# A hybrid decoder layer in three passes over the tokens (128 and the samples, 128, 256) instead of two

## The chip, the cores and the metric

The kernel runs on one core of a Trainium2 chip. The metric is device time in microseconds, the median of several executions. Besides them one execution was profiled; every row shown here is from that one.

The engines are TensorE (PE in the rows, PEld its weight loads, PEq its sequencer), VectorE (DVE), ScalarE (ACT), GpSimd (POOL) and SyncE (SP, which here only starts DMAs).

## What is computed

One layer over 512 prompt tokens and 8 sample tokens, everything in float32, D = 2048. Shortened from the reference:

```python
proj = x @ w_in                                   # z, xbc, dt, u|v, gates
xbc = silu(causal_conv(xbc, conv_state))          # 4 taps
y_a, state = ssd_scan(x, dt, A, B, C, state)      # chunks of 128 tokens, 8 groups of 8 heads
y_a = rms_norm((y_a + d_skip * x) * silu(z))      # by group
u, v = split(gelu(uv));  v = layer_norm(v)
y_b = u * (tril(W_s) @ v + b)                     # within 128-token chunks
merged = g_a * (y_a @ w_branch_a) + g_b * (y_b @ w_branch_b)
h = layer_norm(ALPHA * x + merged @ w_out)
q = h @ w_q                                       # 8 heads, two halves of 128 keys
expert, gate = top16 of the 16 x 16 sums of both halves' top16
act = gelu(einsum('td,thkd->thk', h, peer_u[expert]))     # 128 experts a token
y = layer_norm(ALPHA * h + einsum('thk,thkd->td', gate * act, peer_v[expert]))
```

Of the prompt the final scan state, the last three convolution rows and the last chunk's v are returned too; of every sample the new convolution rows, the new scan state (64 heads x 64 x 128) and v.

## The kernel before

All products with weights are made with the features on the partitions: a weight tile is 128 output features by 2048 inputs, 1 MiB in HBM, and `gemm` (L399) makes 16 matmuls of it against the pass's tokens, which stand side by side in the free dimension. In the profile each such float32 matmul is two records, so a tile is 32. There are 224 tiles, and **each pass over the tokens reads all of them**: pass A has 256 prompt tokens and the 8 samples (264 columns), pass B the other 256.

A pass has three stages with a barrier behind each:

- `ssd` (80 tiles): for each of 8 groups six tiles of B, C and x, four of z; convolution on VectorE, and for each block of 128 tokens `chunk_a` and `chunk_b` on TensorE with `spread_chunk`, `weigh`, `next_state` and `outputs` on VectorE, and `decay` on ScalarE. Then the gating (L1137), its square (ScalarE, L1000), the mean square `rms` (L865) and `finish`. The names conv, weigh and so on stand in the code below.
- `sgu` (32 tiles): v, its layer norm, the spatial product, u.
- `back` (112 tiles): 32 gate tiles, 16 of branch B (`wb`), 32 of branch A (`wa`), 16 of the output (`out`), the layer norm, and 16 query tiles with scores and top-16 selection on VectorE. I call those last 16 tiles the query stage.

**Samples.** In pass A's scan GpSimd updates the samples' states in 64 units of 128 x 512 (eight a group): decay (L1193), B times x (L1195, from the tile BC_bcast), sum (L1197), store to HBM (L1198), product with C (L1201), which VectorE sums in `sum_smp`. The states' loads are issued by GpSimd too (`load`, L1164), two units ahead. BC_bcast is B and C of the samples, turned by TensorE (`turn_bc`, L833), copied by ScalarE (`keep_bc`), written to HBM by GpSimd (L1183) and read back to all partitions (L1185).

**Experts.** Each (block, j) item is a slot: GpSimd gathers 128 rows of peer_u and later 128 rows of peer_v (L250, 1 MiB each), VectorE makes the dot products (L306) and adds the weighted rows (L327). 260 of the 520 slots lie in pass B between its other work, at places that `plan` (L424) writes out; they belong to the tokens of pass A. GpSimd keeps four u rows and four v rows ahead. The other 260 come in the tail with eight rows each.

**Queues.** SyncE issues the weight tiles in the order of the passes (`load_weight`, L390): tile p + 3 after tile p's last matmul, into a ring of three. Between them, in the same order of issue, stand the loads of the decay rows, the stores of y and of the scan state, the branch activations for `wa` (`load_ya`), x (L534) and the keys. An instruction on SyncE that waits holds up all that follow.

## Time and profile before

| | |
|---|---|
| median of 3 runs | 5419.52 us (5419.21 to 5420.57) |
| the profiled execution | 5416.87 us |
| its span | 5414.9 us |
| TensorE busy, mean granted clock | 3608.6 us, 0.828 |
| VectorE busy | 3422.2 us |
| ScalarE busy | 702.4 us |
| GpSimd busy | 2398.3 us |
| DMA | 1672 MB, mean 309 GB/s |
| tables and constants | 0 to 56 us |
| pass A: scan, to the query stage, query stage | 56 to 780, to 1756, to 1938 |
| pass B: scan, spatial stage, gates to output, query stage | 1938 to 2762, to 3085, to 3862, to 4068 |
| tail: 260 expert slots | 4068 to 5415 |

No engine is busy over 67% of the span, because the stages have different limits. The table by stage is the one to read: for each stretch the busy time of each engine, TensorE's granted clock (1 is 2.4 GHz, 0.5 is 1.2 GHz), the share of the 16 DMA engines' time and what they moved.

### The profile page before, as it was taken

To read this page: it belongs to the slowest core of one execution; us is meant where nothing else is said; L and a number is where in the kernel's file an instruction comes from. 1 tells how busy PE (TensorE), PEld (TensorE's weight loads), DVE (VectorE), ACT (ScalarE), POOL (GpSimd) and SP (SyncE) were. 2 spreads that over 40 slices of the span, in tenths; PEclk is the share of its full clock that TensorE was granted. 3 is DMA by queue.
4 is the path that set the end of the run, shared out by engine and by line. 5 is a ranking of instruction groups with operands and counts; after the bars stand their busy time and mean duration, and the time that the engine had idled before them with its cause. 6 is when DMAs were issued, how large, how long until landed. Compare 5 with 4: busy or idle time off the path is not lost. (4 is left out here: it accounts for less than half of the span.)

```text
span 5414.9 us, 43573 instructions
## 1 busy us (share of the span) xinstructions
PE 3608.6 (67%) x16560; PEld 3028.1 (56%) x16560; DVE 3422.2 (63%) x4133; ACT 702.4 (13%) x1501; POOL 2398.3 (44%) x1504
## 2 busy tenths in 40 slices
PE   7999979999999968888778697897940000230000
PEld 5787768888887757667667586786740000000000
DVE  3455531000001859989867665565798999789999
ACT  2232321000000123333311010000100000000000
POOL 3575730000000025545543432443318888778885
PEclk8999989999999989999889898998975555565555
DMA  5565643344444379999989899999749999999998
GB/s 175 192 217 196 210 156 132 133 148 164 164 156 140 126 301 405 421 420 410 421 356 377 351 421 384 389 421 412 307 155 398 420 422 422 422 380 422 422 422 363
DMA packets 275097, 1672.07 MB, mean 309 GB/s; under 512 B 37041, under 2 KB 66225, under 8 KB 81969
## 3 DMA queue, kind: packets, MB, share of 16 engines
q0 software_dynamic: 161920, 1133.78, 51.2%
q1 hardware_dynamic: 112968, 535.51, 26.4%
q8 instruction: 131, 2.15, 0.2%
q14 instruction: 78, 0.63, 0.0%
HBM read 1633.31 MB, written 35.79 MB: 308 GB/s over the span
## 5 line engine op out<-in xcount | busy, mean ns | idle before, releaser
L250 POOL DMA_INDIRECT rows_a<-in_peer_u,expert x384 | 819.0, 2133 | 2182.4 <-POOLq L369 1149.2
L409 PE MATMUL psum<-rows_a,w_ring 128*128 128x264 f32 x7168 | 1625.5, 388 | 24.1 <-PEq L369 18.9
L409 PEld LDWEIGHTS psum<-rows_a,w_ring 128*128 128x128 f32 x7168 | 1367.2, 191 | 265.5 <-issue 30.5
L409 PE MATMUL psum<-x_acts,w_ring 128*128 128x256 f32 x5632 | 1257.4, 384 | 131.0 <-PEq L369 57.5
L409 PEld LDWEIGHTS psum<-x_acts,w_ring 128*128 128x128 f32 x5632 | 1084.0, 193 | 287.9 <-issue 83.4
L306 DVE SCALAR_TENSOR_TENSOR rows_a<-rows_a,h_tokens 128x2048 f32<-128x2048 f32 x384 | 878.7, 2289 | 106.1 <-DMA rows_a<-in_peer_u,expert 75.9
L250 POOL DMA_INDIRECT rows_a<-in_peer_v,expert x384 | 593.3, 1545 | 333.2 <-DVE h_tokens L327 165.1
L327 DVE SCALAR_TENSOR_TENSOR h_tokens<-rows_a,coef,h_tokens 128x2048 f32<-128x2048 f32 x256 | 602.6, 2354 | 79.4 <-issue 73.5
L1744 PE MATMUL psum<-acc,selector 8*128 8x512 f32 x64 | 57.5, 1075 | 683.8 <-DVE rows_a L306 479.0
L1744 PEld LDWEIGHTS psum<-acc,selector 8*128 8x128 f32 x64 | 19.9, 325 | 720.0 <-DVE rows_a L306 485.3
L1019 DVE SCALAR_TENSOR_TENSOR conv_acc<-raw,g_par,conv_acc 128x256 f32<-128x256 f32 x288 | 175.5, 609 | 283.8 <-ACT conv_acc L913 277.0
L327 DVE SCALAR_TENSOR_TENSOR acc<-rows_a,coef,acc 128x2048 f32<-128x2048 f32 x128 | 300.9, 2350 | 32.8 <-issue 30.2
L327 DVE SCALAR_TENSOR_TENSOR h_tokens<-rows_b,coef,h_tokens 128x2048 f32<-128x2048 f32 x128 | 300.9, 2351 | 20.2 <-issue 16.2
L306 DVE SCALAR_TENSOR_TENSOR rows_b<-rows_b,h_tokens 128x2048 f32<-128x2048 f32 x128 | 293.0, 2290 | 27.3 <-DMA rows_b<-in_peer_u,expert 22.6
L286 ACT ACTIVATE gelu<-dots 128x4 f32<-128x4 f32 x130 | 26.7, 205 | 2140.3 <-DVE rows_a L306 1517.1
L250 POOL DMA_INDIRECT rows_b<-in_peer_u,expert x128 | 265.5, 2074 | 81.5 <-issue 37.2
L250 POOL DMA_INDIRECT rows_b<-in_peer_v,expert x128 | 252.9, 1976 | 51.1 <-issue 37.4
L409 PE MATMUL psum<-branch_b,w_ring 128*128 128x256 f32 x1024 | 229.7, 385 | 43.6 <-DMA w_ring<-in_w_tiles 29.1
L409 PEld LDWEIGHTS psum<-branch_b,w_ring 128*128 128x128 f32 x1024 | 197.8, 194 | 72.6 <-issue 43.1
L1622 DVE TENSOR_TENSOR rows_a<-rows_a,psum 128x264 f32<-128x264 f32 x16 | 6.9, 429 | 338.3 <-PE psum L409 338.3
L1631 DVE TENSOR_TENSOR branch_part<-spare,psum 128x264 f32<-128x264 f32 x16 | 6.9, 429 | 214.2 <-PE psum L409 214.2
L409 PE MATMUL psum<-merged,w_ring 128*128 128x256 f32 x512 | 115.2, 384 | 1.8 <-DVE merged L1634 1.8
(368 smaller groups left out, 3024.8 us busy)
## 6 DMA issues: line engine op xcount, KB each, us to landing
w_ring<-in_w_tiles SPq DMA_DIRECT2D x448, 1024.0 KB, 6.3
smp_state<-in_state_ssm POOLq DMA_DIRECT2D x64, 256.0 KB, 5.7
out_ssm_sample<-smp_state POOLq DMA_DIRECT2D x64, 256.0 KB, 3.1
rows_a<-acum_rows_dram SPq DMA_DIRECT2D x16, 512.0 KB, 7.4
BC_bcast<-smp_bc_dram POOLq DMA_DIRECT2D x8, 1024.0 KB, 5.0
branch_b<-acum_rows_dram SPq DMA_DIRECT2D x16, 512.0 KB, 12.4
rows_a<-in_peer_u,expert POOLq DMA_INDIRECT x384, 20.6
rows_a<-in_peer_v,expert POOLq DMA_INDIRECT x384, 21.1
```

The costliest lines, as they stand in the source:

```text
L250: return pool.indirect_dma_start(out=dst, out_offset=None, in_=table, in_offset=bass.IndirectOffsetOnAxis(ap=self.index(s), axis=0))
L286: act.activation(self.ge[:, c], self.dots[:, c], ACT.Gelu).then_inc(self.gelu_done, 1)
L306: dve.scalar_tensor_tensor(out=u, in0=u, scalar=1.0, in1=h, op0=ALU.mult, op1=ALU.mult, accum_out=self.dots[:, s % 8:s % 8 + 1]).then_inc( ...
L327: dve.scalar_tensor_tensor(out=acc, in0=self.vrow[self.slot[s]], scalar=self.coef[:, s % 8:s % 8 + 1], in1=acc, op0=ALU.mult, op1=ALU.add) ...
L409: last = pe.matmul(o, self.w_ring[:, p % RING, k * P:(k + 1) * P], x[:, k, :], start=start and k == 0, stop=stop and k == KB - 1)
L1019: ins = dve.scalar_tensor_tensor(out=ac, in0=r[:, k:k + NP], scalar=w[:, k:k + 1], in1=ac, op0=ALU.mult, op1=ALU.add)
L1622: self.out_of_bank(dve.tensor_tensor(merged[:, m, :], merged[:, m, :], self.bank[(G_WB + m) % 2][:, 0:n], ALU.mult), G_WB + m)
L1631: self.out_of_bank(dve.tensor_tensor(part[:, m % 2, :], ga[:, m, :], self.bank[(G_WA + m) % 2][:, 0:n], ALU.mult), G_WA + m)
L1744: last = pe.matmul(self.bank[c], sel[:, b, :], h_smp[:, 512 * c:512 * (c + 1)], start=True, stop=True)
```

## The change

Everything computed stays the same. The passes are now 128 tokens with the samples (136 columns), 128 tokens, and 256 tokens. I call them A', B' and C'. The weight tiles are read three times. In passes A' and B' the ring has four slots (`w_more` is the fourth), in C' three. The 260 slots within passes are split: 80 in B', 180 in C' (`STEPS_B`, `STEPS_C`: scan per group, v, u, gates, wb, wa, output, layer norm, queries); the tail keeps its 260.

In a pass with one block, `chunk_b` stands behind the last z tile, and VectorE makes the next group's first convolution behind the gating instead of between the sums. The sample states' loads move from GpSimd to SyncE, between the weight tiles, up to four units ahead; the updates stay on GpSimd. The samples' selection is now made in pass B'.

```diff
-RING = 3
-PASSES = 2
+PASS_CHUNKS = ((0, 1), (1, 1), (2, 2))
+PASSES = len(PASS_CHUNKS)
+RINGS = (4, 4, 3)
+RING = max(RINGS)
...
+STEPS_B = (4, 4, 7, 8, 4, 8, 7, 2, 8)
+STEPS_C = (10, 12, 14, 22, 12, 22, 10, 2, 6)
...
-        if p >= PASSES * N_TILES:
-            return
-        if p >= RING:
-            sp.wait_ge(self.w_used, p - RING + 1)
-        sp.dma_start(self.w_ring[:, p % RING, :],
-                     self.a["w_tiles"][ORDER[p % N_TILES]]).then_inc(self.w_in[p % RING], 16)
+        while self.loaded < PASSES * N_TILES and self.loaded - RINGS[self.loaded // N_TILES] <= p:
+            q = self.loaded
+            if self.w_held[q] >= 0:
+                sp.wait_ge(self.w_used, self.w_held[q] + 1)
+            sp.dma_start(self.w_slots[self.w_slot[q]],
+                         self.a["w_tiles"][ORDER[q % N_TILES]]).then_inc(self.w_in[self.w_slot[q]], 16)
+            self.loaded += 1
...
+                def load_smp(v):
+                    if ps.smp and 0 <= v < NU * G:
+                        if v >= 4:
+                            sp.wait_ge(st_out[v % 4], 16 * (v // 4))
+                            sp.wait_ge(prod_read, v - 3)
+                        sp.dma_start(sst[:, v % 4], state_in[GT * (v // NU) + v % NU // 2, :,
+                                                             HB * (v % 2):HB * (v % 2) + HB, :]).then_inc(st_in[v % 4], 16)
+
                 for g in range(2):
                     load_state(g)
+                for v in range(4):
+                    load_smp(v)
                 for g in range(G):
                     for t in range(NT):
-                        self.load_weight(sp, pos(g, t) + RING)
+                        self.load_weight(sp, pos(g, t))
+                        if t >= 3 and NU * g + t - 3 >= 4:
+                            load_smp(NU * g + t - 3)
+                        if t == 0 and g > 0:
+                            load_smp(NU * g - 1)
...
-                    chunk_b(g, 0)
-                    chunk_a(g, 1)
+                    if nc_ > 1:
+                        chunk_b(g, 0)
+                        chunk_a(g, 1)
                     project(g, CT + 3)
+                    if nc_ == 1:
+                        chunk_b(g, 0)
                     if g < G - 1:
                         project(g + 1, 0)
-                    chunk_b(g, 1)
+                    if nc_ > 1:
+                        chunk_b(g, 1)
```

GpSimd in pass A's scan, one unit of the samples' states and the start of the next. Before:

```order
L1193 TENSOR_TENSOR smp_state<-smp_state,dt_smp 128x512
L1195 TENSOR_TENSOR smp_x_dt<-BC_bcast,dt_smp 128x512
L1197 TENSOR_TENSOR smp_state<-smp_state,smp_x_dt 128x512
L1198 DMA out_ssm_sample<-smp_state 128x4x128
L1201 TENSOR_TENSOR smp_out<-smp_state,BC_bcast 128x512
L1164 DMA smp_state<-in_state_ssm 128x4x128
L1193 TENSOR_TENSOR smp_state<-smp_state,dt_smp 128x512
```

The same place in pass A':

```order
L1224 TENSOR_TENSOR smp_state<-smp_state,dt_smp 128x512
L1226 TENSOR_TENSOR smp_x_dt<-BC_bcast,dt_smp 128x512
L1228 TENSOR_TENSOR smp_state<-smp_state,smp_x_dt 128x512
L1229 DMA out_ssm_sample<-smp_state 128x4x128
L1232 TENSOR_TENSOR smp_out<-smp_state,BC_bcast 128x512
L1224 TENSOR_TENSOR smp_state<-smp_state,dt_smp 128x512
```

The state's load is gone from between the units; all else stands as it did. SyncE in a middle group of the scan, from the decay rows' load (acum_rows_dram) to the stores of the group before (branch_acts is y, state_carry the scan state). Before:

```order
L396 DMA w_ring<-in_w_tiles 128x2048 x6
L798 DMA rows_a<-acum_rows_dram 128x1024
L396 DMA w_ring<-in_w_tiles 128x2048 x3
L798 DMA rows_a<-acum_rows_dram 128x1024
L396 DMA w_ring<-in_w_tiles 128x2048
L775 DMA branch_acts<-rows_a 128x4x264
L781 DMA state_carry<-state 128x512
```

In pass A':

```order
L814 DMA rows_a<-acum_rows_dram 128x1024
L407 DMA w_ring<-in_w_tiles 128x2048
L407 DMA w_more<-in_w_tiles 128x2048
L821 DMA smp_state<-in_state_ssm 128x4x128
L407 DMA w_ring<-in_w_tiles 128x2048
L821 DMA smp_state<-in_state_ssm 128x4x128
L407 DMA w_ring<-in_w_tiles 128x2048
L821 DMA smp_state<-in_state_ssm 128x4x128
L791 DMA branch_acts<-rows_a 128x4x136
L797 DMA state_carry<-state 128x512
```

Between two weight tiles there is now a state load, and the second load of decay rows is gone. VectorE in the scan of a pass with expert slots, from the last of the convolutions to the first weighing. Before, in pass B:

```order
L1019 SCALAR_TENSOR_TENSOR conv_acc<-raw,g_par,conv_acc 128x256 x3
L306 SCALAR_TENSOR_TENSOR rows_a,dots<-rows_a,h_tokens 128x2048
L327 SCALAR_TENSOR_TENSOR acc<-rows_a,coef,acc 128x2048
L1044 TENSOR_TENSOR branch_b<-psum,dt_tab 128x512
L1045 TENSOR_TENSOR branch_b<-psum,dt_tab 128x512
L1046 COPY b_tok<-psum 128x128
L1047 TENSOR_TENSOR cb_masked<-psum,triu 128x128
L306 SCALAR_TENSOR_TENSOR rows_a,dots<-rows_a,h_tokens 128x2048
L327 SCALAR_TENSOR_TENSOR acc<-rows_a,coef,acc 128x2048
```

In pass B':

```order
L1055 SCALAR_TENSOR_TENSOR conv_acc<-raw,g_par,conv_acc 128x128 x6
L317 SCALAR_TENSOR_TENSOR rows_a,dots<-rows_a,h_tokens 128x2048
L338 SCALAR_TENSOR_TENSOR acc<-rows_a,coef,acc 128x2048
L1080 TENSOR_TENSOR branch_b<-psum,dt_tab 128x512
L1081 TENSOR_TENSOR branch_b<-psum,dt_tab 128x512
L1082 COPY b_tok<-psum 128x128
L1083 TENSOR_TENSOR cb_masked<-psum,triu 128x128
L1090 COPY chunk_decay<-h_tokens 128x8
L1091 TENSOR_TENSOR h_tokens<-h_tokens,cb_masked 128x1024
```

The weighing follows the spreading without a slot between them, two convolutions stand together, and the convolutions have half the columns.

## Rows read from the trace of the kernel before

**Rows 1.** Busy times by stretch: width, each engine's busy us, granted clock, DMA share, GB/s.

```profile
56.40:779.60 723.20, 661.63 (x3168) 549.97 (x3169) 371.03 (x586) 222.43 (x505) 433.56 (x448) 0.96 0.57 197
779.60:1756.00 976.40, 961.65 (x4326) 819.17 (x4327) 72.18 (x139) 46.72 (x95) 0.00 (x0) 0.99 0.42 148
1756.00:1937.80 181.80, 132.99 (x652) 110.25 (x650) 129.29 (x517) 18.67 (x54) 7.65 (x8) 0.88 0.41 148
1937.80:2762.40 824.60, 667.26 (x3281) 572.60 (x3281) 703.96 (x758) 284.18 (x567) 418.87 (x218) 0.90 0.97 401
2143.00:2246.00 103.00, 87.02 (x429) 74.68 (x428) 93.24 (x102) 37.21 (x77) 55.97 (x31) 0.93 1.02 421
2762.40:3085.30 322.90, 254.87 (x1185) 222.20 (x1185) 215.76 (x190) 28.14 (x67) 134.69 (x80) 0.90 0.92 374
3085.30:3862.40 777.10, 692.46 (x3139) 604.29 (x3139) 493.24 (x429) 46.28 (x81) 303.30 (x196) 0.94 0.98 401
3862.40:4067.80 205.40, 127.29 (x608) 111.45 (x608) 177.23 (x555) 22.36 (x43) 26.09 (x17) 0.81 0.44 159
4067.80:5414.90 1347.10, 87.79 (x128) 25.84 (x128) 1242.54 (x894) 27.03 (x80) 1072.57 (x526) 0.51 0.99 411
```

**Rows 2.** Page, DMA issues: count, KB each, us to landing.

```profile
w_ring<-in_w_tiles SPq DMA_DIRECT2D x448, 1024.0 KB, 6.3
```

**Rows 3.** Timeline of TensorE in pass A and B: start, us, line, what, count.

```profile
962.77 7.29 PE L409 MATMUL psum<-rows_a,w_ring 128*128 128x264 f32 x32
969.89 0.61 PE L1325 MATMUL psum<-rows_a,v_tok 128*128 128x128 f32 x4
970.34 0.38 PE L1315 MATMUL psum<-ident,spare 128*128 128x128 f32 x2
...
2762.37 16.28 PE L409 MATMUL psum<-x_acts,w_ring 128*128 128x256 f32 x64 [19.43 <-PEq L369]
...
2778.92 7.07 PE L409 MATMUL psum<-x_acts,w_ring 128*128 128x256 f32 x32
2785.82 0.59 PE L1214 MATMUL psum<-h_tokens,onesD 128*128 128x256 f32 x2
```

**Rows 4.** Groups by line of VectorE, 2143 to 2658 us: count, busy, mean ns.

```profile
L327 DVE SCALAR_TENSOR_TENSOR acc<-rows_a,coef,acc 128x2048 f32<-128x2048 f32 x71 | 166.9, 2350 | 11.6 <-issue 10.9
L306 DVE SCALAR_TENSOR_TENSOR rows_a<-rows_a,h_tokens 128x2048 f32<-128x2048 f32 x72 | 164.8, 2288 | 3.4 <-DMA rows_a<-in_peer_u,expert 2.5
```

**Rows 5.** Timeline of GpSimd in pass A's scan, from one group to the next.

```profile
326.50 0.79 POOL L1164 DMA_DIRECT2D smp_state<-in_state_ssm  x1
351.70 0.57 POOL L1183 DMA_DIRECT2D smp_bc_dram<-BC_rows  x1 [24.41 <-ACT BC_rows L933]
...
360.10 1.04 POOL L1195 TENSOR_TENSOR smp_x_dt<-BC_bcast,dt_smp 128x512 f32<-128x512 f32 x1 [3.17 <-DMA BC_bcast<-smp_bc_dram]
...
413.30 1.27 POOL L1201 TENSOR_TENSOR smp_out<-smp_state,BC_bcast 128x512 f32<-128x512 f32 x1
```

**Rows 6.** Timeline of TensorE in pass A's scan, between two groups.

```profile
330.43 3.89 PE L865 MATMUL psum<-rows_a,onesG 128*128 128x264 f32 x8 [5.04 <-ACT rows_a L1000]
334.11 15.64 PE L409 MATMUL psum<-rows_a,w_ring 128*128 128x264 f32 x64
```

**Rows 7.** Timeline of VectorE in pass A's query stage: the starts of two heads.

```profile
1877.62 0.49 DVE L153 MAX8 rows_a<-psum 128x8 f32<-128x128 f32 x2
...
1893.77 0.49 DVE L153 MAX8 rows_a<-psum 128x8 f32<-128x128 f32 x2
```

**Rows 8.** Timeline of TensorE: waits for transfers at starts and in pass B.

```profile
1937.75 50.13 PE L409 MATMUL psum<-x_acts,w_ring 128*128 128x256 f32 x224 [48.30 <-DMA x_acts<-in_xT]
...
3472.30 3.75 PE L409 MATMUL psum<-branch_b,w_ring 128*128 128x256 f32 x8 [13.22 <-DMA branch_b<-branch_acts]
...
3734.65 1.22 PE L1214 MATMUL psum<-x_acts,onesD 128*128 128x256 f32 x2 [27.39 <-DVEq L1644]
```

**Rows 9.** Page, costliest groups: weight loads in pass A, busy, mean ns, idle before.

```profile
L409 PEld LDWEIGHTS psum<-rows_a,w_ring 128*128 128x128 f32 x7168 | 1367.2, 191 | 265.5 <-issue 30.5
```

More of the change, by code:

```diff
@@ L105, in __init__ @@
         self.i, self.smp = i, i == 0
[L106 to L108 removed]
+        self.c0, self.nc = PASS_CHUNKS[i]
+        self.np = self.nc * P
+        self.n = self.np + (NS if self.smp else 0)
+        self.first = self.c0 * P
+        self.col = 0 if i == 0 else self.first + NS
         self.pos = N_TILES * i
         self.grp = N_GROUPS * i
[L111 removed]
+        self.rows = [P] * self.nc + ([NS] if self.smp else [])
         self.nb = len(self.rows)
+        self.last = i == PASSES - 1
     def tokens(self, b):
@@ L454, in steps, with span @@
     def steps(self, ps, *key):
-        return self.at[key] if ps.i == 1 else ()
-    def span(self, *names):
-        every = [s for key, r in self.at.items() if key[0] in names for s in r]
-        return range(min(every), max(every) + 1)
+        return self.at.get((ps.i,) + key, ())
+    def span(self, ps, *names):
+        return [s for key, r in self.at.items() if key[0] == ps.i and key[1] in names for s in r]
     def build(self):
@@ L477, in build @@
         passes = [Pass(i) for i in range(PASSES)]
+        ring = [p % RINGS[p // N_TILES] for p in range(PASSES * N_TILES)]
+        last, self.w_slot, self.w_turn, self.w_held, self.loaded = {}, ring, [], [], 0
+        for p, slot in enumerate(ring):
+            self.w_held.append(last.get(slot, -1))
+            self.w_turn.append(ring[:p].count(slot))
+            last[slot] = p
         self.pass_a = passes[0]
@@ L779, in store_state @@
                     sp.wait_ge(fin_ready, g + 1)
-                    dst = self.state_dram[g] if ps.i == 0 else out["ssm_prompt"][g]
+                    dst = self.state_dram[g] if not ps.last else out["ssm_prompt"][g]
                     sp.dma_start(dst, flat(S[:, g % 2])).then_inc(s_out[g % 2], 16)
@@ L1147, in _ @@
                         ex.v_row(pool, s)
-                    for s in self.span("ssd"):
-                        ex.rows(pool, s, 4, 4)
+                if ex:
+                    for s in self.span(ps, "ssd"):
+                        ex.rows(pool, s)
                 if ps.smp:
@@ L1293, in _ @@
                 def _(pool):
-                    for s in self.span("v", "u"):
-                        ex.rows(pool, s, 4, 4)
+                    for s in self.span(ps, "v", "u"):
+                        ex.rows(pool, s)
             @block.tensor
@@ L1473, in _ @@
                 def _(pool):
-                    for s in self.span("gate", "wb", "wa", "out", "ln", "q"):
-                        if s < SLOTS:
-                            ex.u_row(pool, s + 4)
-                        ex.v_row(pool, s + 4 - ex.lag)
+                    for s in self.span(ps, "gate", "wb", "wa", "out", "ln", "q"):
+                        ex.rows(pool, s)
             @block.tensor
@@ L1521, in turn @@
                     c, b = turns[r]
-                    if r < 2 and not ps.smp:
+                    if r < 2 and pick:
                         pe.wait_ge(smp_read, 1)
@@ L1601, in _ @@
                 for c in range(2 * FT):
-                    if not ps.smp and c == 2:
+                    if pick and c == 2:
                         for s in range(2):
@@ L1608, in _ @@
                         o(smp.decode(o, dve, self.iota, 0))
-                    if not ps.smp and c == 6:
+                    if pick and c == 6:
                         dve.wait_ge(smp_exp_done, 1)
@@ L1613, in _ @@
                 for m in range(FT):
-                    if m == 2 and not ps.smp:
+                    if m == 2 and pick:
                         dve.wait_ge(smp_turned, 1)
```

284 lines of the change are left out of this document (139 added, 145 removed).

## The prediction

> **What bounds the kernel now.** I read the stretches of the trace stage by stage first [rows 1]; the reader should see four different limits there. Pass A's scan (723 us): TensorE is busy for 662 us, GpSimd for 434. The rest of pass A up to the query stage (976 us): TensorE 962, nothing else counts. Pass B up to its query stage (825 + 323 + 777 us): DMA share 0.92 to 0.98, and VectorE and TensorE each over 60%. Both query stages belong to VectorE. The tail (1347 us) is DMA alone, at 0.99. So TensorE's columns are worth time in pass A only, bytes are worth time in pass B and the tail, and the change cuts columns and adds bytes.
>
> **Units.** A weight tile is 1 MiB [rows 2], an expert slot two gathers of 1 MiB, and at full share the engines move 421 GB/s (the stretch 2143:2246 [rows 1]), so 2.49 us per MiB. A tile takes TensorE 969.89 - 962.77 = 7.12 us at 264 columns and 2785.82 - 2778.92 = 6.90 us at 256 [rows 3]: 32 records of 223 and 216 ns, 0.83 ns a column and 3 ns over. At 136 columns I get 117 ns and **3.74 us a tile**, at 128 columns 110 ns and **3.52 us**. The trace has no long stream of 128 columns against 128x128 weights, but a short one: four records from 969.89 to 970.34, 112 ns each [rows 3]. A slot costs VectorE 2.29 + 2.35 minus overlaps, 4.5 us [rows 4].
>
> The Trainium skill weighs against this row (TensorE: Matmul & The Clock Gate, Back-to-back issue gap): in a stream the spacing is set by weight load and matmul together, and for 128 columns it gives about 81 ns where the matmul alone would be 56. Scaled by that ratio, as an estimate, a record would be 159 ns, a tile 5.1 us and the whole some 6100 us; no row here shows such a gap: the records at 969.89 are 112 ns apart.
>
> **Pass A' (128 tokens and the samples), scan.** It stays with GpSimd. One group runs from the first product with BC_bcast at 360.10 to the end of the last at 414.57, 54.5 us [rows 5]; the change takes away eight state-load issues of 0.79 us [rows 5] and leaves 48.2. They go to SyncE, which waits there for the store and the sum of the unit four back, with weight tiles and the decay rows queued behind, and TensorE behind those; the four tiles ahead (15 us) cover the wait for a unit of 6 us, so I price it at nothing (uncovered, 6 us a group, 48 in all). Between groups GpSimd idles from 327.3 to 351.7, then needs 8.4 us for the broadcast [rows 5]. That idle time is a chain: last sum, gating, square, mean square on TensorE at 330.43, projections from 334.11, 7.8 us each partly at the half clock [rows 6], copy. With half the columns it is 2.1 + 0.6 + 1.9 + 5.2 + 3.7 + 2.3 = 15.8 us, including 1.5 for a clock at 1.2 GHz after TensorE's longer idle (after 19.4 us idle, two tiles took 16.28 against 14.0 [rows 3]). Scan: first four tiles and start 19, broadcast 8.4, 8 x 48.2, 7 x 24.2, end 15: **597 us, minus 126**. TensorE's 80 tiles alone would be 300; that gain does not come.
>
> **Pass A', rest.** 128 tiles to the query stage: 976.4 - 128 x 7.12 leaves 65, of which half the 39 for means and transposes stays, 26 of idle time, and 7 for loads that 3.7 us of a tile cover less well: 479 + 19 + 26 + 7 = **531, minus 445**. In the query stage VectorE needs 1893.77 - 1877.62 = 16.15 us a head for two blocks [rows 7]; for one block half would be 8.1, but chained small operations don't halve: 10. TensorE needs 9.2. Eight heads, 5 at the end, and the 27 us for x beside the first eight gathers (the 48.3 us wait at 1937.75 less VectorE's 21 [rows 8]): **112, minus 70**. Pass A' ends at 56 + 597 + 531 + 112 = 1296.
>
> **Pass B' (128 tokens, 80 slots), all new.** Weights come once more: 224 MiB. Scan group: 10 tiles and 4 slots are 18 MiB, with the small ones 20.2 MB: 48 us. TensorE is busy 0.845 of a group of 99.6 in pass B, 84 [rows 1], of which 69 are tiles; so here 35.2 and half of the other 15, 43. VectorE 18 + 15 (half of the 27 that 0.905 x 99.6 - 63 leaves in pass B). Before, 41.9 MB make 99.6 us, and 824.6 - 8 x 99.6 = 28 for start and end. So 8 x 49 + 30 = 422. Spatial stage: 54 MiB and 2 more, 139, and of the 39 by which the old one exceeds its 284 I keep 24: 163. Gates to the output: 96 tiles, 27 slots and 4 MiB of activations and keys, 154 MiB, are 383; TensorE's own path is 340 + 7 for the tiles and means, and the waits in series are branch activations (13.2 us at 3472.30), x (27.4 at 3734.65 [rows 8]) and the normalisation (12): x and the branch activations come in as many pieces as before, only shorter ones, beside gathers of 8 KB pieces, so I let these loads keep their length, while the tiles that cover them halve. I take 425. Query stage: VectorE 80 + 8 x 4.5 = 116, at the 0.87 it reached before, and the barrier: 139. Start with x: 9. Sum **plus 1158**; bounds 1000 (384 MiB and 18 MB, DMA never idle) and 1300 (TensorE's path and the gathers in turn).
>
> On that sharing the Trainium skill (DMA: Bandwidth & Descriptors, Queues, rings and completion order) says that each DMA engine takes turns between its rings packet by packet; short pieces then wait behind long ones. The 27.4 us at 3734.65 agree with that, though no row shows the packets themselves.
>
> **Pass C' (256 tokens, 180 slots instead of 260).** Scan group: 10 slots, 30 MiB: 80 us; TensorE 84 as above; VectorE 45 + 27 = 72. Three limits close together, 84 a group: 8 x 84 + 33 = 705 (before 825). Spatial stage: 214 for DMA, TensorE 221 + 25, and waits 37: 283 (323). Gates to output: TensorE 662 + 14, normalisation 22, and the waits above 42: 740 (777). Query stage: 6 slots for 9: 193 (205). **1921, minus 209**; bounds 1742 (TensorE's busy time in the four stretches of pass B [rows 1]) and 2130 (pass B's own).
>
> **Tail.** 260 items remain as before: 1347, unchanged, at a DMA share of 0.99 [rows 1].
>
> **Sum.** 1296 + 1158 + 1921 + 1347 = 5722 of span, and 2 around it (5416.9 for 5414.9): 5724; the median of the runs is 3 above the profiled one. **5725 us, 5.6% slower.**
>
> **Rivals.**
> 1. *The waits are covered (the other side).* Pass B' runs at DMA's 1000 and pass C' at TensorE's 1742: 1296 + 1000 + 1742 + 1347 = 5385, 0.6% faster. The mechanism is that four tiles and eight rows in flight carry DMA over every barrier, normalisation and query stage. It decides from 30 us of such waits in the two passes together; the old pass B alone has 2130 less DMA's 1919 (744 MiB and 28 MB), 211, and the two query stages would keep some 70. 4%.
> 2. *A weight load sets TensorE's pace.* A load shows 191 ns on average [rows 9]; not overlapped with each other the loads give 6.1 us a tile: 300 more in pass A' (128 x 2.36), about 430 in pass B': 6450. Against it: four records, each with its load, in 0.45 us [rows 3]. 5%.
> 3. *Pass C' gains nothing*, since VectorE's order of slots and scan steps, not DMA, sets pass B's pace (it is busy 93 of 103 us [rows 1]): 2130, total 5930. For it: VectorE's share; against: DMA share 1.02 in the same row. 8%.
> 4. *Pass B's scan is a chain*: with one block a group, weighing, both products, gating and the next convolution follow one another, with four slots of 4.5 us among them, 62 us instead of 49: 5830. 10%.
> 5. *The change does not do what it says* (slots fall together at one place, the third pass reads weights late behind SyncE's state loads): the rows of the order show even steps, 2%, some 5800.
>
> **Numbers.** My forecast holds 71%, between 5590 and 5860; rival 4 lies inside. Range 5590 to 5860 for 8 in 10: left out are most of rivals 1, 2 and 3. About 0.2% can be told from no change: faster 0.03, same 0.01, slower 0.96.
>
> **What would show it.** In the new profile: pass A' scan with GpSimd stretches of 48 us and gaps of 24; tiles of 3.7 us with records 117 ns apart after it; pass B' about 1150 with DMA share over 0.85 until its query stage; pass C' scan groups of 84 us with TensorE over 0.9; a tail of 1347. Wrong is most easily pass B' (its waits in series) and how far pass C' gets away from its old pace.

## The result, and the profile after

The changed kernel takes **5734.94 us**, median of four executions (5720.78 to 5740.13), beside 5420.05 us for the kernel before (5419.21 to 5421.02): a ratio of 1.0577, 95% interval 1.0558 to 1.0596. It is 5.8% slower. The profiled execution took 5720.78 us with a span of 5718.5 us; the forecast for that execution was 5724.

The busy times by stretch of the changed kernel, with the columns of [rows 1] (from:to and width in us, busy us and instructions of TensorE, weight loads, VectorE, ScalarE and GpSimd, granted clock, DMA share, GB/s). The first three lines are pass A' (scan, to the query stage, query stage and the load of x), the next four pass B' (scan, spatial stage, gates to output, query stage and x), then four of C', then the tail:

```profile
56.40:699.20 642.80, 370.58 (x2840) 355.15 (x2840) 194.72 (x482) 144.70 (x408) 381.40 (x384) 0.77 0.60 212
699.20:1219.60 520.40, 503.42 (x4272) 501.43 (x4272) 46.92 (x133) 34.46 (x95) 0.00 (x0) 0.99 0.77 272
1219.60:1325.20 105.60, 76.31 (x609) 70.30 (x609) 79.37 (x322) 15.24 (x50) 7.65 (x8) 0.86 0.54 195
1325.20:1719.70 394.50, 339.13 (x2953) 326.95 (x2953) 257.60 (x394) 166.97 (x423) 102.23 (x58) 0.95 1.00 409
1719.70:1890.40 170.70, 133.37 (x1136) 131.35 (x1137) 71.11 (x95) 19.90 (x59) 43.30 (x22) 0.90 0.87 345
1890.40:2310.90 420.50, 369.77 (x3138) 364.79 (x3139) 158.62 (x202) 25.90 (x55) 101.71 (x56) 0.95 0.95 384
2310.90:2460.60 149.70, 71.55 (x561) 70.49 (x561) 119.75 (x351) 15.10 (x37) 33.58 (x18) 0.74 0.72 266
2460.60:3175.10 714.50, 647.65 (x3280) 556.76 (x3280) 572.88 (x661) 267.97 (x547) 310.07 (x160) 0.95 0.92 376
3175.10:3466.90 291.80, 255.42 (x1185) 223.30 (x1185) 150.24 (x143) 27.65 (x63) 98.09 (x52) 0.93 0.79 313
3466.90:4183.10 716.20, 686.84 (x3137) 601.67 (x3137) 339.24 (x290) 36.92 (x67) 248.73 (x132) 0.98 0.87 345
4183.10:4371.50 188.40, 125.92 (x608) 110.35 (x608) 163.34 (x545) 20.21 (x40) 16.05 (x13) 0.83 0.39 141
4371.50:5718.50 1347.00, 86.97 (x128) 25.74 (x128) 1242.93 (x894) 26.36 (x79) 1073.06 (x526) 0.51 0.99 411
```

**Where the time went.** Pass A took 1881 us before [rows 1], A' takes 1269: 612 less. Pass B took 2130, C' takes 1911: 219 less. B' is new: 1135. That is 304 more, and the spans differ by 5718.5 - 5414.9 = 303.6. The tail is the same 1347. What the reader is to see line by line: in the first, no engine is near the width, and GpSimd is busiest (381 of 643); in the second TensorE is busy for 503 of 520; in the lines of B' the DMA share is 1.00, 0.87, 0.95 and then 0.72 in the query stage; and in C' TensorE is busy for 91, 88 and 96% of the first three stretches, where it was busy for 81, 79 and 89% of the same stretches of pass B [rows 1].

Against the terms of the sum:

| | forecast | measured |
|---|---|---|
| A' scan | 597 | 642.8 |
| A' to the query stage | 531 | 520.4 |
| A' query stage and x | 112 | 105.6 |
| B' scan | 422 | 394.5 |
| B' spatial stage | 163 | 170.7 |
| B' gates to output | 425 | 420.5 |
| B' query stage and x | 148 | 149.7 |
| C' scan | 705 | 714.5 |
| C' spatial stage | 283 | 291.8 |
| C' gates to output | 740 | 716.2 |
| C' query stage | 193 | 188.4 |
| tail | 1347 | 1347.0 |

The sum is only 4 us off because A' scan's 46 too many meet a net 50 too few in the others. So the first line is what the experiments had to explain.

**One group of A' scan.** The timeline of GpSimd in the changed kernel (start, us, line, what, idle time before with what ended it), the counterpart of [rows 5]:

```profile
292.78 1.27 POOL L1232 TENSOR_TENSOR smp_out<-smp_state,BC_bcast 128x512 f32<-128x512 f32 x1
...
308.56 0.61 POOL L1214 DMA_DIRECT2D smp_bc_dram<-BC_rows  x1 [14.51 <-ACT BC_rows L968]
313.56 0.58 POOL L1216 DMA_DIRECT2D BC_bcast<-smp_bc_dram  x1 [4.39 <-DMA smp_bc_dram<-BC_rows]
...
323.37 1.04 POOL L1226 TENSOR_TENSOR smp_x_dt<-BC_bcast,dt_smp 128x512 f32<-128x512 f32 x1 [7.88 <-DMA BC_bcast<-smp_bc_dram]
```

From the store of B and C (308.56) to the first product that uses them (323.37) it takes 14.8 us; in [rows 5] the same way took 8.4, with the second DMA issued at

```profile
354.98 0.58 POOL L1185 DMA_DIRECT2D BC_bcast<-smp_bc_dram  x1 [2.71 <-DMA smp_bc_dram<-BC_rows]
```

Both halves are longer: 5.0 us until the second DMA is issued (3.3 before) and 9.8 after that (5.1 before). Over all eight groups the means are 5.5 (3.5 before) and 8.8 (5.1 before). The page's table of DMA issues for the changed kernel (count, KB each, median us from issue to landing) says so too; before, the first of these lines had 5.0:

```profile
BC_bcast<-smp_bc_dram POOLq DMA_DIRECT2D x8, 1024.0 KB, 8.9
...
w_ring<-in_w_tiles SPq DMA_DIRECT2D x560, 1024.0 KB, 8.6
w_more<-in_w_tiles SPq DMA_DIRECT2D x112, 1024.0 KB, 7.0
```

I split a group in three on GpSimd's timeline, since its instructions follow one another there without another engine between: *broadcast* (issue of the store of B and C to the first product), *updates* (first product to the issue of the last state's store) and *rest* (to the next group's store of B and C; it holds the last product with C and the chain through gating, mean square and two tiles). *Group* is the time from one group's store of B and C to the next group's. Means of eight groups (of seven for rest and group, so the parts add up to the group only within 0.4), us:

| kernel | broadcast | updates | rest | group |
|---|---|---|---|---|
| before | 8.7 | 52.2 | 26.4 | 87.4 |
| changed | 14.4 | 46.6 | 17.5 | 78.5 |
| forecast | 8.4 | 46.2 | 17.8 | 72.4 |

The other two terms are right to half a microsecond. (The forecast's 48.2 ran to the end of the last product, 2 us behind its store, so 46.2 and 15.8 + 2 here.) The broadcast alone is 6 us longer than forecast, and eight times that is 48, for 46 missed. (Single broadcasts scatter, from 12.6 to 15.9 us in the changed kernel and from 8.1 to 9.6 before.)

**A tile of 136 columns.** TensorE's timeline in the changed kernel, the counterpart of [rows 3]:

```profile
959.19 3.87 PE L422 MATMUL psum<-rows_a,w_more 128*128 128x136 f32 x32
962.90 11.28 PE L422 MATMUL psum<-rows_a,w_ring 128*128 128x136 f32 x96
974.02 3.87 PE L422 MATMUL psum<-rows_a,w_more 128*128 128x136 f32 x32
```

962.90 - 959.19 = 3.71 us a tile, 116 ns a record; 3.74 and 117 were forecast. The three tiles behind it take 974.02 - 962.90 = 11.12, the same pace. This is the row that decides rival 2, with its 6.1 us a tile.

### The profile page after: what moved, and what is told of

Read it like the earlier page. It is cut to its first block and busy times, and to the rows that moved or that the text cites. A ratio compares the mean times of both kernels' runs of the same rounds, so it can differ in the third digit from the quotient of the medians.

```text
span 5718.5 us, 60009 instructions
## 1 busy us (share of the span) xinstructions
PE 3690.5 (65%) x23920; PEld 3351.3 (59%) x23920; DVE 3413.7 (60%) x4576; ACT 807.9 (14%) x1932; POOL 2417.4 (42%) x1440
## 5 line engine op out<-in xcount | busy, mean ns | idle before, releaser
L422 PE MATMUL psum<-x_acts,w_ring 128*128 128x256 f32 (+1 forms) x9984 | 1790.1, 341 | 267.7 <-DMA w_ring<-in_w_tiles 100.6
L261 POOL DMA_INDIRECT rows_a<-in_peer_u,expert x384 | 913.5, 2379 | 2467.6 <-DVE rows_a L317 1717.2
L422 PEld LDWEIGHTS psum<-x_acts,w_ring 128*128 128x128 f32 x9984 | 1604.0, 196 | 436.5 <-issue 207.0
L317 DVE SCALAR_TENSOR_TENSOR rows_a<-rows_a,h_tokens 128x2048 f32<-128x2048 f32 x384 | 877.9, 2287 | 34.7 <-PEq L380 13.2
L422 PE MATMUL psum<-rows_a,w_ring 128*128 128x136 f32 x5376 | 665.4, 286 | 22.8 <-PEq L380 17.0
L422 PEld LDWEIGHTS psum<-rows_a,w_ring 128*128 128x128 f32 x5376 | 657.4, 196 | 34.0 <-issue 33.0
L1055 DVE SCALAR_TENSOR_TENSOR conv_acc<-raw,g_par,conv_acc 128x128 f32<-128x128 f32 (+1 forms) x432 | 173.4, 401 | 286.0 <-ACT conv_acc L948 275.3
L422 PE MATMUL psum<-branch_b,w_ring 128*128 128x256 f32 (+1 forms) x1664 | 304.2, 344 | 21.4 <-DMA branch_b<-branch_acts 19.7
L422 PEld LDWEIGHTS psum<-branch_b,w_ring 128*128 128x128 f32 x1664 | 271.9, 194 | 50.2 <-issue 17.0
L422 PE MATMUL psum<-rows_a,w_more 128*128 128x136 f32 x1792 | 216.9, 279 | 0.0
L422 PEld LDWEIGHTS psum<-rows_a,w_more 128*128 128x128 f32 x1792 | 211.7, 190 | 0.4 <-issue 0.4
```

The source lines that it names most:

```text
L261: return pool.indirect_dma_start(out=dst, out_offset=None, in_=table, in_offset=bass.IndirectOffsetOnAxis(ap=self.index(s), axis=0))
L317: dve.scalar_tensor_tensor(out=u, in0=u, scalar=1.0, in1=h, op0=ALU.mult, op1=ALU.mult, accum_out=self.dots[:, s % 8:s % 8 + 1]).then_inc( ...
L422: last = pe.matmul(o, w[:, k * P:(k + 1) * P], x[:, k, :], start=start and k == 0, stop=stop and k == KB - 1)
L1055: ins = dve.scalar_tensor_tensor(out=ac, in0=r[:, k:k + np_], scalar=w[:, k:k + 1], in1=ac, op0=ALU.mult, op1=ALU.add)
```

## The experiments

Each kernel is the changed one with the edit shown, unless the text says that it is the kernel before. Ratios are to the kernel before on the same chip (medians 5418.0, 5420.5 and 5419.5 us there). The profiled execution of the changed kernel is the fastest of its four, 14 us under their median, so a difference between medians and one between profiled spans or stretches can lie apart by that much; where they do, both are given.

### The broadcast, with less traffic beside it

```diff
-            sp.dma_start(self.w_slots[self.w_slot[q]],
-                         self.a["w_tiles"][ORDER[q % N_TILES]]).then_inc(self.w_in[self.w_slot[q]], 16)
+            cols = 128 if 4 <= q < N_SSD else WCOLS
+            sp.dma_start(self.w_slots[self.w_slot[q]][:, 0:cols],
+                         self.a["w_tiles"][ORDER[q % N_TILES]][:, 0:cols]).then_inc(self.w_in[self.w_slot[q]], 16)
```

> The changed kernel, whose weight loads of pass A's scan (after the first four tiles) bring only 128 of 2048 columns; what is computed there is wrong, all else is as it was. Theory (the broadcast of B and C through HBM takes 14.4 us instead of 8.4 because weight tiles now come twice as fast and share the DMA engines with it): from the issue of the write to the first product 8 to 9 us, pass A's scan 643 to about 598, the whole 45 us shorter. Rival 1 (the state loads on SyncE slow it): 14 us as before, no change. Rival 2 (weights are late for TensorE there): the gap between the groups' last product and the write, 15.5 us, shrinks too and the scan falls below 590.

Measured: 5681.38 us, ratio 1.0491 [1.0472, 1.0510], 54 less than the changed kernel by the medians and 46 by the profiled spans. The kernel loads a sixteenth of each weight tile of that scan after the first four. The line of A' scan, and GpSimd's timeline at a group's boundary:

```profile
59.60:660.60 601.00, 356.54 (x2840) 344.77 (x2841) 199.08 (x482) 144.85 (x409) 382.06 (x384) 0.79 0.33 102
```

```profile
296.94 0.61 POOL L1215 DMA_DIRECT2D smp_bc_dram<-BC_rows  x1 [15.21 <-ACT BC_rows L969]
299.49 0.58 POOL L1217 DMA_DIRECT2D BC_bcast<-smp_bc_dram  x1 [1.95 <-DMA smp_bc_dram<-BC_rows]
...
307.34 1.04 POOL L1227 TENSOR_TENSOR smp_x_dt<-BC_bcast,dt_smp 128x512 f32<-128x512 f32 x1 [5.91 <-DMA BC_bcast<-smp_bc_dram]
```

The scan falls from 642.8 to 601.0. The parts of a group are 9.0, 46.7 and 17.5, the group 73.1 us: the broadcast gives back 5.4 of the 6, the updates and the rest do not move. So the weight traffic is what stretched the broadcast, and the mean DMA share of the stretch does not show it: it was only 0.60 in the changed kernel (0.57 before). What counts is what is in flight when the broadcast is issued. My reading of the timelines is this: TensorE stands idle for 25 us a group, and then takes eight tiles within 31 us (298.92 to 330.15 in the changed kernel), with the broadcast's 308.56 to 323.37 in the middle of them. Their successors' loads, 1 MiB each 3.7 us instead of each 7.1, fall on it.

This is where a rule of the Trainium skill fits (DMA: Bandwidth & Descriptors, Queues, rings and completion order): each DMA engine takes turns between its rings packet by packet, so GpSimd's broadcast shares with SyncE's weights. The trace agrees as far as it goes: 9.0 us with thin weights, 14.4 with whole ones. No row shows the packets' order.

### The state loads back on GpSimd

SyncE's loads go, and GpSimd issues them two units ahead, as in the kernel before:

```diff
-                for v in range(4):
-                    load_smp(v)
...
-                        if t >= 3 and NU * g + t - 3 >= 4:
-                            load_smp(NU * g + t - 3)
...
+                            load(v + 2)
```

> The changed kernel with the state loads back on GpSimd, two units ahead. Theory (the GpSimd loop sets the scan's pace): 8 x 6.3 us come back, pass A's scan 643 to about 690, the whole 45 to 50 us longer than the changed kernel, about 5782; the broadcast still takes 13 to 15 us. Rival (the state loads in SyncE's queue are what makes the broadcast slow): the broadcast goes back to 9 us and the whole is unchanged within 10 us.

Measured: 5750.70 us, 1.0615 [1.0591, 1.0638], only 16 more than the changed kernel (28 by the profiled spans), where the theory had 45 to 50.

```profile
58.00:725.10 667.10, 362.98 (x2840) 348.78 (x2841) 184.16 (x482) 144.96 (x409) 429.20 (x448) 0.76 0.58 204
```

The parts of a group are 12.5, 51.7 and 17.2, the group 81.0. The updates are 5.1 us longer, less than the 6.3 of eight issues. But the broadcast is 1.9 us shorter, below the theory's 13 to 15. Single ones scatter from 10.3 to 16.5 here; that the difference is real is borne out by the page's median from issue to landing of BC_bcast, 7.5 us here and 8.6 to 9.5 in the changed kernel and the five others that keep both its weight tiles in this scan and SyncE's state loads. So the rival has a part of the truth: the state loads share in crowding the broadcast, beside the weights. The likely reason is that SyncE may have four state loads in flight at a group's start and GpSimd two; no run parts it further. So the moved loads are worth 2.5 us a group, not the 6 they cost as instructions: part of the gain was paid in the broadcast. The median moved by 16 where the scan moved by 24; the intervals of both ratios reach 10 to 13 us to either side, so nothing hangs on the other 8.

### The same move in the kernel with two passes

Here the kernel before gets SyncE's state loads, at the same places between its weight tiles:

```diff
+                        if t >= 3 and NU * g + t - 3 >= 4:
+                            load_smp(NU * g + t - 3)
...
-                            load(v + 2)
```

> The kernel before with one part of the change alone: the samples' state loads issued by SyncE between the weight tiles. Theory (the scan of pass A is a loop of GpSimd's units and a chain between groups, so eight issues of 0.79 us a group count in full until TensorE's 83 us a group bind): the group goes from 88.6 to 83 us, the whole 30 to 50 us shorter, 5370 to 5390. Rival (TensorE sets the pace of this scan already, being busy for 662 of 723 us): within 10 us of before, 5410 to 5425.

Measured: 5442.59 us, 1.0040 [1.0026, 1.0054]. It is slower by 0.4%, with an interval clear of 1; my theory had the sign wrong. The scan's line (723.2 wide before, [rows 1]), and GpSimd between units:

```profile
56.70:797.80 741.10, 661.70 (x3168) 548.64 (x3168) 345.71 (x586) 221.92 (x505) 391.71 (x384) 0.94 0.55 192
```

```profile
295.62 1.87 POOL L1197 TENSOR_TENSOR smp_state<-smp_state,dt_smp 128x512 f32<-128x512 f32 x1 [0.63 <-DMA smp_state<-in_state_ssm]
...
310.26 1.03 POOL L1197 TENSOR_TENSOR smp_state<-smp_state,dt_smp 128x512 f32<-128x512 f32 x1 [1.04 <-DMA smp_state<-in_state_ssm]
...
321.51 1.03 POOL L1197 TENSOR_TENSOR smp_state<-smp_state,dt_smp 128x512 f32<-128x512 f32 x1 [3.86 <-DMA smp_state<-in_state_ssm]
```

GpSimd has eight instructions fewer a group (391.7 us busy, 433.6 before) and is no faster: 9.3, 53.7 and 26.4, the group 89.3 us, 87.4 before. SyncE's own timeline says why, here before the third of those waits:

```profile
314.49 0.33 SPq L396 DMA_DIRECT2D w_ring<-in_w_tiles  x1
314.92 0.38 SPq L805 DMA_DIRECT2D smp_state<-in_state_ssm  x1
```

A state load stands on SyncE behind a weight tile's load, and that one waits for a buffer, which comes free once in 7.1 us; a unit of updates takes 6. From 100 to 790 us SyncE's weight loads wait for TensorE for 587 us in all, and the profile shows no wait of its state loads themselves. So the loads come late and GpSimd waits for them, 48 us in 28 waits, 0.6 to 3.9 us in the rows above. In A' a tile is 3.7 us, the loads run ahead (GpSimd never waits for one there), and the updates are 46.6 for 46.2 forecast. The fourth weight buffer is not the reason: with three in every pass (the last experiment) the updates are 46.6 too. **The prediction priced this queue at nothing for A' and that holds, because of A's halved tiles; at 264 columns the same edit costs some 22 us.**

### What GpSimd's loop is worth

The product of states and C goes to VectorE, which sums it anyway; GpSimd only signals the state. (In its place GpSimd now waits for a group's last sum before it overwrites BC_bcast, since VectorE reads that too, and in the kernel with two passes also before it reloads a state; these lines are not shown.)

```diff
-                            pool.tensor_tensor(sout[:, v % 2], s, Cb[:, b0:b0 + HB, :], ALU.mult).then_inc(prod_ready, 1)
+                            pool.sem_inc(prod_ready, 1)
...
                         dve.wait_ge(prod_ready, v + 1)
+                        o(dve.tensor_tensor(sout[:, v % 2], sst[:, v % 4], Cb[:, HB * (u % 2):HB * (u % 2) + HB, :],
+                                            ALU.mult))
```

> The changed kernel with the product of the samples' states and C on VectorE (before its sum there) instead of on GpSimd. Theory (the GpSimd loop sets pass A's scan): a unit 1.25 us shorter, 8 x (10 - 1) us, pass A's scan 643 to about 572, the whole 65 to 75 us shorter, 5665. Rival (the loop's pace is the state loads or SyncE's order by now): the scan stays over 620.

Measured: ratio 1.0428 [1.0409, 1.0448], that is some 5652 us, and 5651.25 in the profiled execution: about 80 less than the changed kernel (69 by the profiled spans), the cheapest gain found in it. (One of its four executions took 13.4 ms and is left out; I know no reason for it in the kernel.)

```profile
56.60:623.00 566.40, 366.87 (x2840) 352.31 (x2840) 242.66 (x546) 144.70 (x408) 302.38 (x320) 0.81 0.68 240
```

The parts are 14.7, 38.0 and 16.1, the group 68.8. Nearly all that GpSimd loses comes off the scan (9.7 us a group, 76 in the stretch), though VectorE gains 48 us of work. GpSimd's chain is the bound of A' scan.

In the kernel with two passes:

> The kernel before (two passes, state loads on GpSimd) with the product of the samples' states and C on VectorE. Theory (GpSimd's loop sets the scan of pass A also at 264 columns, and TensorE's 83 us a group bind next): the group 88.6 to about 83, the whole 20 to 45 us shorter than before, 5375 to 5400. Rival (TensorE and VectorE set that scan): within 10 us of before or slower.

Measured: 5412.95 us (eleven executions), 0.9986 [0.9977, 0.9995].

```profile
56.60:774.10 717.50, 661.68 (x3169) 550.34 (x3169) 402.40 (x648) 222.74 (x505) 355.82 (x384) 0.96 0.58 199
```

The parts are 8.7, 48.6 and 29.7, the group 87.1: the updates are 3.6 us shorter and the rest 3.3 longer. With 264 columns TensorE has 662 us to do in 717, and what GpSimd leaves is mostly taken by its wait for the copy of B and C behind TensorE's projections: 182.3 us over the seven boundaries, 164.9 before. So the very edit that is worth 80 us at 136 columns is worth 7 at 264. It is the only kernel of this study that beats both, by 0.14% (interval 0.05 to 0.23%).

### What pass B' costs, by its slots

```diff
-STEPS_B = (4, 4, 7, 8, 4, 8, 7, 2, 8)
-STEPS_C = (10, 12, 14, 22, 12, 22, 10, 2, 6)
+STEPS_B = (0, 0, 0, 0, 0, 0, 0, 0, 0)
+STEPS_C = (14, 20, 20, 32, 16, 32, 16, 3, 9)
```

> The changed kernel with no expert slots in pass B and all 260 in pass C. Theory (pass B is bound by DMA's bytes with slots, and without them by TensorE's 3.5 us a tile with the same waits in series): pass B 1135 to about 1000, its scan 394 to 360; pass C becomes the old pass B, 1911 to 2130; the whole about 80 us longer than the changed kernel, 5815. Rival (a pass of 128 tokens is a chain of single steps, whatever the slots): pass B stays over 1100, the whole over 5900.

Measured: 5757.46 us, 1.0616 [1.0600, 1.0632], 23 more than the changed kernel by the medians and 42 by the profiled spans, where the theory had 80. Pass B' without slots, in three stretches (scan, spatial stage, the rest):

```profile
1328.00:1675.50 347.50, 330.31 (x2953) 323.05 (x2953) 125.93 (x296) 145.30 (x400) 3.74 (x4) 0.97 0.82 296
1675.50:1813.00 137.50, 132.36 (x1136) 131.31 (x1137) 22.04 (x59) 19.56 (x57) 0.00 (x0) 0.97 0.72 259
1813.00:2279.50 466.50, 421.36 (x3699) 418.83 (x3699) 111.29 (x432) 26.13 (x72) 0.00 (x0) 0.96 0.74 265
```

B' is 951.5 us, C' (now with 260 slots) 2133. And the other way:

```diff
-STEPS_B = (4, 4, 7, 8, 4, 8, 7, 2, 8)
-STEPS_C = (10, 12, 14, 22, 12, 22, 10, 2, 6)
+STEPS_B = (6, 7, 10, 12, 6, 12, 11, 2, 12)
+STEPS_C = (8, 9, 10, 17, 9, 17, 7, 2, 5)
```

> The changed kernel with 120 expert slots in pass B and 140 in pass C. Theory (from 80 slots on pass B is bound by DMA's bytes, 5.0 us a slot, while pass C nears TensorE's time): pass B 1135 to about 1325, pass C 1911 to about 1860, the whole 120 to 150 us longer than the changed kernel, 5865. Rival (pass C is still set by its slots on VectorE and DMA, 5.5 us each as between 180 and 260): pass C falls by 200 us and the whole stays within 20 us of the changed kernel.

Measured: 5881.16 us, 1.0851 [1.0835, 1.0868].

```profile
1328.70:1807.30 478.60, 357.18 (x2953) 343.51 (x2953) 328.44 (x446) 172.42 (x431) 175.38 (x93) 0.89 1.00 410
...
2645.40:3352.30 706.90, 646.68 (x3280) 554.53 (x3281) 501.31 (x609) 267.31 (x543) 248.38 (x128) 0.96 0.85 333
```

The first is B' scan, the second C' scan. B' is 1317 us, C' 1883. Put together, in us:

| slots in B' / C' | B' | C' | sum |
|---|---|---|---|
| 0 / 260 | 951 | 2133 | 3084 |
| 80 / 180 | 1135 | 1911 | 3046 |
| 120 / 140 | 1317 | 1883 | 3200 |

A slot in B' costs (1135 - 951) / 80 = 2.3 us at first and (1317 - 1135) / 40 = 4.5 from there on, close to the 5.0 that its two gathers take at full DMA share. A slot in C' costs (2133 - 1911) / 80 = 2.8 above 180 and 28 / 40 = 0.7 below, where TensorE sets the pace: taking 40 slots out shortens its scan only from 714.5 to 706.9. The split of the change is the best of the three measured, and no other can help: even an empty B' costs 951, and with B' empty C' is as slow as pass B was (2130). To come out even with the kernel before, B' and C' together would have to take 2742 (2130 and the 612 that A' saves). If a pass gets no shorter by more slots, fewer than 80 in B' leave at least 951 + 1911 = 2862, and more than 80 at least 1135 + 1742 = 2877, the 1742 being TensorE's busy time in pass B [rows 1]. The old pass B is reproduced to 3 us by C' with 260 slots, which also says that nothing else in the new program slowed it.

### Bytes or waits in pass B'

```diff
-            sp.dma_start(self.w_slots[self.w_slot[q]],
-                         self.a["w_tiles"][ORDER[q % N_TILES]]).then_inc(self.w_in[self.w_slot[q]], 16)
+            cols = 128 if N_TILES <= q < 2 * N_TILES else WCOLS
+            sp.dma_start(self.w_slots[self.w_slot[q]][:, 0:cols],
+                         self.a["w_tiles"][ORDER[q % N_TILES]][:, 0:cols]).then_inc(self.w_in[self.w_slot[q]], 16)
```

> The changed kernel, whose weight loads of all of pass B bring only 128 of 2048 columns; what is computed from there on is wrong. Theory (bytes set pass B's pace): pass B 1135 to about 985, near the 951 that it takes without slots, the whole 150 us shorter, 5585. Rival (slots standing in line on VectorE and waits in series set it): pass B over 1080, the whole over 5680.

Measured: 5604.20 us, 1.0339 [1.0323, 1.0355], 131 less than the changed kernel by the medians and 115 by the profiled spans. The kernel loads a sixteenth of every weight tile of B'. Pass B' in the same three stretches:

```profile
1329.90:1675.50 345.60, 326.19 (x2953) 319.38 (x2953) 257.57 (x394) 167.05 (x423) 105.56 (x62) 0.97 0.68 245
1675.50:1835.20 159.70, 132.50 (x1136) 131.30 (x1137) 71.12 (x95) 19.91 (x59) 43.34 (x22) 0.92 0.47 172
1835.20:2350.30 515.10, 428.29 (x3699) 426.36 (x3699) 278.20 (x552) 41.04 (x92) 138.39 (x74) 0.91 0.51 184
```

B' is 1020.4 us, between what theory and rival had: of 1135 the bytes are worth 115, and neither has it whole. The scan falls by 49, to 345.6, the width that it has with all its bytes and no slots (347.5): TensorE's pace. There VectorE has room for the slots and only DMA's time was at stake; rival 4, the chain in the scan, is dead with it, for the slots cost nothing once the bytes are gone. The spatial stage falls by 11 of 171. The rest falls from 570.2 to 515.1 but stays 49 above the kernel without slots: there slots cost time of their own at a DMA share of 0.51, and in the spatial stage too (159.7 for 137.5 at 0.47). That they stand in series with the stage's work is my reading; no run parts them.

TensorE's timeline at the output tiles of B', in the changed kernel, shows the pace of DMA itself:

```profile
2272.01 3.81 PE L422 MATMUL psum<-merged,w_more 128*128 128x128 f32 x32 [0.89 <-DMA w_more<-in_w_tiles]
...
2276.96 3.81 PE L422 MATMUL psum<-merged,w_ring 128*128 128x128 f32 x32 [0.92 <-DMA w_ring<-in_w_tiles]
```

4.95 us from tile to tile, twice the 2.49 of a MiB: beside each weight tile goes a MiB of gathered rows (from 2266 to 2296 us the DMA share is 1.01). TensorE alone needs 3.8 for a tile and its two records of the mean, and waits for the rest, 0.9 us before each.

### The fourth weight buffer

```diff
-RINGS = (4, 4, 3)
-RING = max(RINGS)
+RINGS = (3, 3, 3)
+RING = 4
```

> The changed kernel with three weight tiles in flight in every pass (the fourth place stays allocated and unused). Theory (a tile of 128 columns takes TensorE 3.5 to 3.7 us and a load lands 7 to 9 us after its issue, so two tiles of cover are too few, and SyncE's state loads are covered by the fourth): pass A's rest and pass B wait for tiles, 40 to 120 us longer in all, most of it in pass B; pass A's scan within 10 us. Rival (the fourth tile covers nothing, because bytes set pass B and GpSimd pass A's scan): within 15 us of the changed kernel.

Measured: 5782.12 us, 1.0666 [1.0647, 1.0686], 47 more than the changed kernel by the medians and 66 by the profiled spans. A' scan and B' scan:

```profile
57.90:702.30 644.40, 370.84 (x2841) 353.62 (x2841) 193.61 (x482) 145.08 (x409) 381.85 (x384) 0.79 0.60 211
1335.80:1754.50 418.70, 345.81 (x2952) 333.44 (x2952) 257.54 (x394) 167.08 (x423) 102.33 (x58) 0.94 0.97 386
```

A' scan is the same (its groups too: 14.6, 46.6 and 17.3), so the fourth buffer is not what crowds the broadcast; what is left is the pace at which buffers come free. B' is 1194 instead of 1135, 59 of the 66 us: 24 of them in the scan, at a DMA share of 0.97 instead of 1.00, and 30 from the gates to the output (450.0 for 420.5). The rest of A' is 8 longer. Both fit the theory, which had most of it in pass B. With four tiles in flight DMA hardly pauses in B' scan, with three it does; so much of rival 1's mechanism is there.

## Why the prediction was right

**What bounds what.** It rested on one reading of [rows 1]: columns are worth time in pass A only, and bytes in pass B. The first held: A' to the query stage is 520.4 of 531. The second held in B' scan, whose DMA share is 1.00 and which gives back 49 us when the weights' bytes go; in all of B' the weights' bytes are worth 115 of 1135, and TensorE's way 951. C' is held by TensorE after 80 slots less, and no more is to be had there (0.7 us a slot).

**Tile pace.** 3.71 us measured, 3.74 forecast, from records of 223 ns for 264 columns and four of 112 ns for 128. Rival 2 (6.1 us a tile) had the mean of 191 ns of a weight load [rows 9] for it. That mean is 196 after, at 116 ns from record to record, so the loads overlap one another:

```profile
L422 PEld LDWEIGHTS psum<-rows_a,w_ring 128*128 128x128 f32 x5376 | 657.4, 196 | 34.0 <-issue 33.0
```

By the Trainium skill (TensorE: Matmul & The Clock Gate, Back-to-back issue gap) weight load and matmul together set the spacing in a stream, which the prediction scaled to an estimate of 159 ns a record. This trace does not agree: 116 ns, and the measurement decides.

**A' to the query stage** was 11 less than the 531. The prediction read 26 us of idle time into the old stretch and kept them, with 7 for loads. [rows 1] has TensorE busy for 961.65 of 976.40, so idle for 15; after, it is 503.42 of 520.40, 17 idle.

**A' scan: the term that was mis-sized.** The structure was right: GpSimd's loop sets it (removing work there took 76 us from it), TensorE idles, the chain between groups with the last product is 17.5 for 17.8, the updates 46.6 for 46.2. The step that failed is "then needs 8.4 us for the broadcast", taken over from [rows 5] unchanged. It measured 14.4, since the 8.4 was a price under one tile in 7.1 us; with a tile in 3.7 the weight loads crowd it, and thin weights brought it back to 9.0. I had kept the lengths of x and the branch activations in pass B' for such sharing, and not looked at this row in A'. Those two were priced too high by it, as Pass B' below shows.

**Moved state loads.** "I price it at nothing", of SyncE's queue, was right (46.6 for 46.2). What it didn't see is that the updates gain 5.1 us and not 6.3, that more than a third of that is given back through the broadcast (1.9), and that in the kernel with two passes the edit costs.

**Pass B'.** 1158 forecast, 1135 measured. The scan is 27 less: 8 x 49 was the DMA bound and 30 for start and end; the whole stretch ran at a share of 1.00, with no start or end of its own to be seen. The other three are within 8, but in the gates to output that was luck. Its parts, 347 us for TensorE and 53 of waits in series, come to 400, and the 425 was taken with no term for the rest. TensorE is busy for 370. Of its 51 idle us the branch activations take 9.5 (13.2 kept) and x 9.4 (27.4 kept), and 23 go to waits for weight tiles. So x and the branch activations did not keep their length. In C', where x has all its bytes, its wait is as short:

```profile
2232.94 0.80 PE L1245 MATMUL psum<-x_acts,onesD 128*128 128x128 f32 x2 [9.44 <-DVEq L1677]
...
4056.61 1.22 PE L1245 MATMUL psum<-x_acts,onesD 128*128 128x256 f32 x2 [8.51 <-DVEq L1677]
```

The bounds hold too: 1000 for bytes alone, where the kernel without slots needs 951 for TensorE's way alone, and the two together 1135. Rival 4 expected a chain of 62 us a group; 394.5 / 8 is 49.3 with everything.

**Pass C'.** 1921 forecast, 1911 measured: scan 10 more, spatial stage 9 more, gates to output 24 less: beside TensorE's busy time I had 64 for the normalisation and the waits, and 716.2 - 686.8 = 29 is all the time it was idle there, with 11 more of busy time. The wait for x is 19 shorter than the one kept. Rival 3, no gain at all (2130), is what 260 slots give.

**Rival 1**, the other side, needed B' at 1000 and C' at 1742. They were 135 and 169 above; it decides at 30 of the sum. And even with the weights' bytes nearly gone in B', the pass takes 1020.

**The sum** was closer than its terms (5722 for 5718.5), since 46 too few in A' scan met a net 50 too many in the others; that is luck. The 5725 given for the median missed it by 10: the median of the changed kernel stands 14 us above its profiled execution, and only 3 were allowed. Its four executions spread over 19 us and those of the kernel before over 2, which no row explains.

What stays open: why B' without slots needs 163 us beyond 224 tiles of 3.52 (its query stage is held by VectorE, and x, the normalisation and three barriers stand in series, but no run parted them); how weights and state loads share the broadcast's 6 us, of which thinner weights give back 5.4 and fewer state loads in flight 1.9, since no run has both; and whether a kernel of three passes with the product on VectorE and thinner traffic at the broadcast would come near the kernel before. By the sums it would not: 80 and 46 of 315.

## What to carry to other kernels

A pass that reads all weights again has a floor, TensorE's way through all tiles (951 us here), and pays only if the passes beside it lose more than that; find for each pass what its columns, bytes and slots are worth at the margin (4.5 and 0.7 us a slot in neighbouring passes) before the work is split. A latency read from the trace, like a round trip through HBM, is a price under that traffic: when the change halves the time between the transfers beside it, price the round trip again, whatever the mean DMA share says. And the same edit has another size, even another sign, where another engine sets the pace: moved loads cost 22 us and a moved product gained 7 with 264 columns, where they gained some 20 (16 to 28, by the measure taken) and 80 with 136.

## What the hardware showed unexpectedly

- A store of B and C and its broadcast back to all partitions took 8.7 us at one weight tile in 7.1 us, 14.4 at one in 3.7, and 9.0 with the weights cut to a sixteenth, at mean DMA shares of 0.57, 0.60 and 0.33.
- The granted clock of a stretch overstates what idle time costs TensorE. Its timeline at the same group boundary of A' scan (counterpart of [rows 6]):

```profile
296.95 2.18 PE L896 MATMUL psum<-rows_a,onesG 128*128 128x136 f32 x8 [24.80 <-ACT rows_a L1036]
298.92 8.00 PE L422 MATMUL psum<-rows_a,w_ring 128*128 128x136 f32 x64
306.76 0.38 PE L864 MATMUL psum<-ident,rows_a 128*8 128x128 f32 x2
```

  After 24.8 us without work the eight records of the mean square take 1.97 us instead of 0.93 (8 x 116 ns), at a granted clock of 0.50, the lower of the two levels, and the two tiles behind them 7.84 instead of 7.42: 1.5 us, as forecast. But this is the cheapest of the seven boundaries between groups. Reckoned in the same way they cost 1.5 to 3.0 us, 2.3 on average and 16 in the scan. In every group the clock is down a second time, after 5.6 to 10 us without work:

```profile
337.97 1.98 PE L888 MATMUL psum<-rows_a 128*64 128x128 f32 x16 [7.82 <-DVE rows_a L1092]
339.88 2.08 PE L891 MATMUL psum<-rows_a,b_tok 128*128 128x512 f32 x2
```

  Until the next tile at 341.75 these 18 records take 3.78 us at 0.50; their like in the kernel before took 1.99 (386.27 to 388.26). This second loss stands beside GpSimd's updates and not in the chain. The granted clock of 0.77 (0.96 before) looks like much more than both, but idle time counts in it: from 350 to 365 us it is 0.65, with TensorE busy for 0.5 us.
